# A state-space block with its norm moved to token rows, its scan cut into quarters, its skip term folded into the tables, and its outputs evicted through gelu

## The reference

```python
for i in range(2):
    x = x + 0.5 * swiglu(rmsnorm(x, ffn1_norm[i]), ffn1_w_in[i], ffn1_w_out[i])
    h = rmsnorm(x, mix_norm[i])
    x = x + (s5_mixer(h, ...) if i == 0 else hgrn2_mixer(h, ...))
    x = x + cross_attend(rmsnorm(x, xattn_norm[i]), mem_k[i], mem_v[i], ...)
    x = x + 0.5 * swiglu(rmsnorm(x, ffn2_norm[i]), ffn2_w_in[i], ffn2_w_out[i])
# s5_mixer: 64 groups of 16 channels, each driving a 64-dim complex diagonal state
h_t = lam_bar * h_{t-1} + b_bar @ u_t
y_t = gelu(real(c @ h_t) + d * u_t)
out = (y @ w_glu)[:, :1024] * sigmoid((y @ w_glu)[:, 1024:])
```

## Time and profile before

| | us |
|---|---|
| median of 3 runs | 2545.58 |
| the profiled execution, its own time | 2546.63 |
| its span | 2544.9 |
| PE busy | 2462.6 (97% of the span) |
| DVE busy | 1258.5 |
| ACT busy | 853.5 |
| POOL busy | 612.7 |

### The profile page before, as it was taken

One profiled execution on the slowest core, in us unless ns is written; L12 is line 12 of the kernel. 1 busy time (PEld: TensorE's weight loads), 2 busy tenths in 40 slices (PEclk: granted clock), 3 DMA queues, 4 the chain that ended last, 5 costly groups with the idle time before them and its releaser, 6 DMA issues.

```text
span 2544.9 us, 49720 instructions
## 1 busy us (share of the span) xinstructions
PE 2462.6 (97%) x21037; PEld 2370.9 (93%) x21037; DVE 1258.5 (49%) x1764; ACT 853.5 (34%) x1228; POOL 612.7 (24%) x604
## 2 busy tenths in 40 slices
PE   6999999799999999999999999999998999999999
PEld 6999999688976999999999999999998959999998
DVE  4553543854555543344543244466776565442443
ACT  3332221443222322222333133266664233221222
POOL 5579948241201100001211010331122203000003
PEclk8999999899999999999999999999999999999999
DMA  8255444363354333233443333333332543332332
GB/s 163 84 165 128 123 123 147 104 201 107 110 196 133 91 91 105 79 90 100 143 117 114 99 92 107 92 86 101 94 103 63 200 158 89 93 101 86 90 99 76
DMA packets 479670, 289.16 MB, mean 114 GB/s; under 512 B 22352, under 2 KB 467024, under 8 KB 478480
## 3 DMA queue, kind: packets, MB, share of 16 engines
q1 hardware_dynamic: 473760, 280.66, 37.6%
q0 software_dynamic: 848, 1.89, 0.7%
q10 hardware_dynamic: 4896, 4.20, 0.5%
HBM read 258.86 MB, written 27.85 MB: 113 GB/s over the span
## 4 chain that ended last, share of the span: by engine, by line
PE 91%; DVE 4%; ACT 2%; DMA 1%; issue 1%; POOL 1%; SPq 0%; DVEq 0%; ACTq 0%; POOLq 0%
PE lin L2670 76%; PE mis L2237 3%; DMA raw<-in_ffn_w_in_dram 1%; PE mis L2358 1%; DVE w_lo L1668 1%; DVE rstd L1681 1%; PE mis L2343 1%; PE mis L2293 1%; PE lin L2358 1%; PE mis L2523 1%; PE mis L2515 0%; PE lin L2601 0%; POOL w_lo L975 0%; DVE a_lo L1674 0%; DVE kc L1726 0%
## 5 line engine op out<-in xcount | busy, mean ns | idle before, releaser
L2670 PE MATMUL lin<-a_hi,w_hi 128*128 128x260 f32 x3584 | 1023.9, 286 | 18.9 <-DVE w_lo L1668 15.0
L2670 PE MATMUL lin<-a_lo,w_hi 128*128 128x260 f32 x3584 | 1015.8, 283 | 0.0
L2670 PE MATMUL lin<-a_hi,w_lo 128*128 128x260 f32 x3584 | 1015.2, 283 | 0.0
L2670 PEld LDWEIGHTS lin<-a_hi,w_hi 128*128 128x128 f32 x3584 | 677.1, 189 | 25.6 <-issue 12.8
L1668 DVE TENSOR_TENSOR w_lo<-raw,w_hi 128x1024 fp32r<-128x1024 f32 (+1 forms) x328 | 499.1, 1522 | 403.8 <-ACT w_hi L1239 403.4
L2670 PEld LDWEIGHTS lin<-a_hi,w_lo 128*128 128x128 f32 x3584 | 678.2, 189 | 0.0
L2670 PEld LDWEIGHTS lin<-a_lo,w_hi 128*128 128x128 f32 x3584 | 677.9, 189 | 0.2
L2670 PE MATMUL lin<-h_hi,w_hi 128*128 128x260 f32 x2016 | 570.1, 283 | 4.6 <-DVE h_lo L1898 1.7
L2670 PE MATMUL lin<-h_hi,w_lo 128*128 128x260 f32 x2016 | 569.3, 282 | 0.0
L2670 PE MATMUL lin<-h_lo,w_hi 128*128 128x260 f32 x2016 | 568.5, 282 | 0.0
L1239 ACT ACTIVATE w_hi<-raw 128x1024 fp32r<-128x1024 f32 (+1 forms) x328 | 364.5, 1111 | 320.1 <-PE lin L2670 300.0
(11 more groups left out here) (453 smaller groups left out, 2586.9 us busy)
## 6 DMA issues: line engine op xcount, KB each, us to landing
raw<-in_ffn_w_in_dram SPq DMA_DIRECT2D x176, 512.0 KB, 3.8
raw<-in_ffn_w_out_dram SPq DMA_DIRECT2D x64, 704.0 KB, 4.6
kc<-in_cache_mem_k_dram SPq DMA_DIRECT2D x32, 512.0 KB, 5.3
vc<-in_cache_mem_v_dram SPq DMA_DIRECT2D x16, 1024.0 KB, 8.6
raw<-in_hg_w_in_dram SPq DMA_DIRECT2D x32, 512.0 KB, 4.1
raw<-in_xattn_w_kv_dram SPq DMA_DIRECT2D x16, 512.0 KB, 4.3
raw<-in_s_w_glu_dram SPq DMA_DIRECT2D x16, 512.0 KB, 4.0
raw<-in_xattn_w_q_dram SPq DMA_DIRECT2D x16, 512.0 KB, 4.0
```

The lines of the kernel that those rows point to most:

```text
L2670: ins = pe.matmul(lin[:, j, half, 0:HT], w[:, j, k, :], x[:, k, cols], start=k == 0 and u == 0, stop=k == kt - 1 and u == 2)
```

## The change

- **Norm.** ACT packs tiles 0 to 6 from `xT` times gain, without the reciprocal, while `ffn1_out1` still runs (a new `sZ` of six tiles, and `sZ6`); DVE packs tile 7. ACT squares tile 7 and DVE adds it to POOL's sum. PE sums over channels into one column per step, so that the sums stand by token rows (80 x 8), after the sixth X group. Root and reciprocal are taken on 80 x 8, and the reciprocal is multiplied in when an X group is emptied (DVE six groups of eight, ACT two, in four pieces each).
- **Order.** X, U of the first half; X of the second; then FU of the first half, h0, U and FU of the second. Waits for all groups at the start of U and FU become waits for the groups that are read.
- **Scan** in four quarters with a signal for each; hfin comes later; Y(4,1) goes to ACT.
- **Skip term.** POOL makes `dD`, d on a 16-wide diagonal, and PE adds it to each K group with four more products of 16 columns per group. y needs no u any more: ACT empties y groups through gelu into `u32`.
- **kv.** The eight products with `w_lo` come last in a step, and only they wait for it (both layers). POOL's `kv_low` waits for the reciprocal.
- **Transfers.** Three tables instead of two are fetched ahead; the rotation tables, kv loads and memory tiles are fetched in another order. Root and gelu tables are loaded ahead by ACT on a spare element.

The list of groups:

```diff
+    sZ = at("sZ", [P, 6, CS, UC], F32, o_al)
+    sZ6 = at("sZ6", [P, CS, UC], F32, o_small + 2048 + 3 * TILE)
+    X_OWNER = ("dve", "act", "dve", "dve", "act", "dve", "dve", "dve")
     for hf in range(2):
-        made += [("X", (4 * hf + f, e), "act") for f in range(4) for e in range(2)]
...
+        made += [("X", (4 * hf + f, e), X_OWNER[2 * f + e]) for f in range(4) for e in range(2)]
         if hf == 0:
+            made += [("U", q, "dve" if q % 2 else "act") for q in range(8)]
+    made += [("FU", q, "dve" if q % 2 else "act") for q in range(8)] + [("h0", 0, "dve")]
+    made += [("U", 8 + q, "act") for q in range(8)] + [("FU", 8 + q, "act") for q in range(8)]
+    made += [("Y", (u, g), "act") for u in range(4) for g in range(2)]
+    made += [("y", (f, e), "act") for f in range(4) for e in range(2)]
```

SP:

```diff
-                sp.wait_ge(s5_z, 1)
-                rotation_in(0, "S")
-                kv_memory(0)
-                sp.wait_ge(s5_fill, S5G.at("X", (7, 1)) + 1)
+                sp.wait_ge(s5_fill, 1)
                 rotation_in(1, "C")
                 rotation_in(1, "S")
-                for c in (2, 3):
-                    kv_load(0, c)
+                sp.wait_ge(sums_done, s5_norm + 1)
+                rotation_in(0, "S")
+                kv_load(0, 2)
+                sp.wait_ge(s5_fill, S5G.at("X", (5, 1)) + 1)
+                rotation_in(0, "C")
+                kv_load(0, 3)
+                kv_memory(0)
```

ACT:

```diff
+                for f in range(7):
+                    act.wait_ge(used[f % 2], p0 + f // 2 + 1)
...
+                    act.activation(z[:, :, 0:NC], xT[:, f, 0:SEQ].rearrange("p (n s) -> p s n", s=CS), ACT.Copy, scale=gain)
...
+                act.activation(t2[:], xT[:, KD - 1, :], ACT.Square).then_inc(s5_packed, 1)
+                kv_split(0, 1)
                 act.wait_ge(sums_done, s5_norm + 1)
...
+                        act.activation(u32[:, f, 0:SEQ].rearrange("p (n s) -> p n s", s=CS)[:, :, 4 * e:4 * e + 4],
+                                       bank[:, 0:4 * YC].rearrange("p (t n) -> p n t", t=4)[:, 0:NC, :],
+                                       ACT.Gelu_apprx_tanh).then_inc(s5_void["act"], 1)
+                        if e:
+                            hidden({5: range(3), 6: range(3, 5), 7: range(5, KD)}.get(f, ()))
```

DVE:

```diff
+                        dve.tensor_tensor(dst, src, scale.unsqueeze(2).unsqueeze(3).to_broadcast([UC, 4, 8, SC]), ALU.mult)\
```

PE:

```diff
-                pe.wait_ge(kv_lo, v + 1)
+                pe.wait_ge(kv_hi, v + 1)
...
+                for u, (w, x) in enumerate(((kv_his[l], m_hi[l]), (kv_his[l], m_lo[l]), (kv_los[l], m_hi[l]))):
+                    if u == 2:
+                        pe.wait_ge(kv_lo, v + 1)
+                    for k in range(KD):
...
+                            ins = pe.matmul(bank[0:2 * SC, u * P:u * P + SC], ident[:, 2 * SC * u:2 * SC * (u + 1)],
+                                            dD[:, a, :], start=False, stop=True)
...
-                sums(s5_norm)
-                pe.wait_ge(root_done, s5_norm + 1)
...
+                    for k in range(CS):
+                        pe.matmul(mis[0:NC, 2, k:k + 1], acc[:, 0:SEQ].rearrange("p (n s) -> p s n", s=CS)[:, CS - 1 - k],
+                                  ones[:, 0:1], start=True, stop=True)
+                    pe.matmul(mis[NC:UC, 2, 0:CS], accS[:].rearrange("p a b -> p (a b)"), ones[:, 0:CS],
+                              start=True, stop=True).then_inc(sums_done, 1)
...
-                            pe.wait_ge(s5_scanned, 1 + u // 4)
+                            pe.wait_ge(s5_scanned, 1 + u // 2)
```

More of the change, by code:

```diff
@@ L763, in s5_loads @@
                 sp.wait_ge(s5_rot_out, 16 * 4)
-                rotation_in(0, "C")
-                for q in range(2):
+                for q in range(3):
                     s5_tables_in(q)
@@ L991, in body @@
                             continue
-                        if last and j == 1 and r == NORMS - 1:
+                        if last and j == 1 and r in (s5_norm, NORMS - 1):
                             continue
@@ L995, in body @@
                         ins = pool.tensor_tensor(acc[:], acc[:], sqt[:], ALU.add)
-                        if last and j == (0 if one or r == NORMS - 1 else 1):
+                        if last and j == (0 if one or r in (s5_norm, NORMS - 1) else 1):
                             ins.then_inc(squares_done, 1)
@@ L1457, in s5 @@
                         kv_tokens(0, KV - 1)
-                        gelu(5)
-                        hidden(range(3))
                         continue
@@ L1463, in s5 @@
                         continue
-                    if what == "X" and a[0] >= 4 and a[1] == 0:
-                        for f in (4, 5) if a[0] == 4 else range(a[0] + 1, min(a[0] + 2, KD)):
-                            packed(f)
                     act.wait_ge(s5_fill, q + 1)
@@ L1469, in s5 @@
                     if what == "X":
[L1470 to L1472 removed]
+                        if a[0] >= 4:
                             act.wait_ge(s5_fill, G.first("U") + 8)
[L1474 to L1477 removed]
+                        dst, src, scale = x_rows(a, bank)
+                        for u in range(4):
+                            ins = act.activation(dst[:, u], src[:, u], ACT.Copy, scale=scale[:, u:u + 1])
+                        ins.then_inc(s5_void["act"], 1)
+                        continue
+                    if what == "U":
                         dst, src = sU[:, 4 * a:4 * a + 4, :], bank[:, 0:4 * UC].rearrange("p (g n) -> p g n", g=4)
@@ new lines, in turn @@
+                    dve.tensor_tensor(x[:, 0], a[:, 0], b[:, 1], ALU.subtract if back else ALU.add)
+                    link(dve.tensor_tensor(x[:, 1], a[:, 1], b[:, 0], ALU.add if back else ALU.subtract))
+                for f in range(2):
+                    turn(f, False)
+                    q_ = slice(f * nj // 2, (f + 1) * nj // 2)
+                    j_ = slice(half * nj + f * nj // 2, half * nj + (f + 1) * nj // 2)
+                    for e in range(2):
+                        x = sFH[:, e, j_, :].rearrange("p j n -> p (j n)")
+                        link(dve.tensor_tensor_scan(x, rotR[:, q_].rearrange("p j n -> p (j n)"), x, 0.0, ALU.mult, ALU.add))
+                    if half == 0 and f == 1:
+                        dve.tensor_copy(rotR[:, :, 2:NC + 1], decay[:, nj:].unsqueeze(2).to_broadcast([P, nj, NC - 1]))
+                    turn(f, True)
+                    link(dve.tensor_copy(hfin[:, :, j_], sFH[:, :, j_, NC]))
+                    link(dve.tensor_copy(sFH[:, :, j_, NC:YC], hs0[:, :, :, j_].rearrange("p e b j -> p e j b")))
+                    dve.nop().then_inc(s5_scanned, 1)
```

219 lines of the change are left out of this document (102 added, 117 removed).

## The result

The change takes 2526.59 us (median of 4 runs, 2524.20 to 2528.02) against 2545.86 (4 runs, 2544.36 to 2548.33) for the kernel before on the same chip: ratio 0.9922, 95% interval 0.9907 to 0.9936. That is 19.3 us less. A second series of the same kernel gave a ratio of 0.9942 (0.9928 to 0.9957), so the gain is known as some 15 to 20 us and not to the microsecond.

The account below looks back on a forecast made before the run. PE was taken as the bound, busy 2462.6 of 2544.9 us. Front -14.3, K products +2.4 and back +1.6 sum to -10.3 us: 2535.3 us for a median, own range 2531 to 2540, whole range 2527 to 2543.

Parts of the forecast that it names:

- the list of steps: Front, feed-forward's end to first kv product: X, sums, U, FU timed in turn; at full clock kv starts 18.3 us earlier.
- Front, -14.3: From the feed-forward's last product to the first kv product: 18.3 us saved at full clock, less 4 for a clock fall.
- a fall that lasts for about 8 us costs 4: Front: PE, fed in drops from 449.5 to about 461, drops to the lower clock for about 8 us, losing 4.
- K products, +2.4: K groups: 64 added matmuls in the trace, at FU's pace of 0.037 us each, count in full on PE: +2.4 us.
- Back, +1.6: From the first kv product to the start of `glu`: net loss of 1.6 us, from -2 to +8.
- kv(2): -1.9: Third kv step, back: with the `w_lo` products last, 16 matmuls cover 1.9 of the 2.03 us wait.
- y(0) to y(3), +1.0: Back, ahead of Y(4): ACT empties y through gelu at 0.5 us each; PE's wait of 0.64 becomes 1.6.
- SP's tables, +1.4: Back: SP is held by a kv load, so Y(3)'s tables may come late like Y(2)'s: +1.4 us (-0.4 to +6).
- The end, +1.1: Behind the last Y: ACT alone needs 4.5 us until `glu` may start, against 3.4 when shared with DVE.
- the quarters themselves bring nothing: Scan in quarters, back: no gain, since the scan is off the path and three kv steps (11 us) hide Y(0)'s quarter.
- Of the rivals, the first: No fall of the clock and the queues hold: -19.1 us in all, 2526.5 us; chance 0.2.
- The second, low clock throughout: Clock stays low through the front, which gains only 4.0 us: total 0, 2545.6 us; chance 0.1.

## Why the prediction was wrong

The main mechanism was right: the chain behind the feed-forward goes, X starts at once, and the end moves by what the front loses. The steps that failed are the back, where the sum has a loss and the kernel gained, and in the front the cost of the fall of the clock and the list of steps. All three terms of the sum were mis-sized on the slow side.

- **Front, -14.3; measured -18.0, and about -17 in the mean of nine profiles** (against 46.90; the other profile with the front of before has 48.27, at 27.3 us of low clock). The sum stood for a front of 32.6 from start to start: 28.6 for the steps at full clock and 4.0 for the fall. Measured were 28.0 and a stall of 0.86 that nothing foretold. Of the 28.0 some 1.5 are the fall, which was 3.4 us long and not 8, and 26.5 the steps (estimates, with 0.43 us for each us of half clock). So "a fall that lasts for about 8 us costs 4" was too dear by 2.5, of which 2.0 is the length. That is luck: in the mean of nine profiles it was 7.6 us, and would then cost 3.3. The list was too long by 2.1. Its first steps weren't: the sums took 2.2 us, not 1.3, and the scale came 5.6 after the feed-forward's end, not 5.2. But the second U took 3.4 us, not 4.3, and the second FU 4.6, not 4.9. I took 0.5 for ACT to empty a U group; it lasts 0.44 and starts every 0.32. The rest of the 2.1 lies between the scale and the first FU product, where the clock falls and the estimate is rough.
- **K products, +2.4; measured +1.8.** FU's pace, 0.037, was too dear for 16 columns: 0.029.
- **Back, +1.6; measured -4.1,** which is the largest miss. kv(2): -1.9 was right for the wait, but 0.62 for the keys showed behind it: -1.4. y(0) to y(3), +1.0: nothing. I took 0.5 for a gelu of half a tile; it starts every 0.26. SP's tables, +1.4: 0.4 less in this profile, and 0.7 to 1.0 of wait in five of the other ten traces whose transfers are the change's. A wait of 0.32 for evicted values, which the sum left out, is gone too. The end, +1.1: -0.4 up to the first `glu` product and -1.5 behind it. I added up ACT's work as one row and left out that DVE, once it no longer empties y, runs `h_lo` ahead. The 0.61 us between the first weight tiles of `glu` stood in the trace of before, just behind the window that I had read.

Points of the forecast's own list: X within 0.3 us, right; scale 5 us after, 5.6; first kv product near 481.4, at 478.90; the low stretch, 3.4 us in place of 8; K groups +0.23, not 0.3; `w_lo`'s wait gone, right; Y(4) 1 us later, wrong. Two readings in it are off by a little: by their own shares (0.73 and 0.59) the clock before fell at 449.5 and 480.2, not at 449.7 and 480.4, so what is called 3 us of idleness at full clock was 2.8. The list has the two FU blocks at 4.65 and 4.9 us, where its row gives 4.7 for each; that moves the sum by 0.2. The remark that "the quarters themselves bring nothing" was wrong: the sum did not rest on it, but without the quarters some 60% of the gain would be lost. Of the rivals, the first had the time right, with -18.0 + 1.8 - 4.1 behind it in place of its -18.3 + 1.2 - 2.0, so it came out for a part of its reasons: the clock did fall, for 3.4 us. The second, low clock throughout, was refuted: between 457 and 461 PE ran only transposes, and the clock rose from 0.50 to 0.98 at 460. The Trainium skill (TensorE: Matmul & The Clock Gate, Part 4: PE-mode transpose) has full clock not engage there; this trace disagrees again. Of the others, SP's queue cost at most 1.0 us, the K products pipelined, and the scale was not late.

## What to carry to other kernels

Charge a fall of the clock a little under half its length where PE sets the pace (0.43 and 0.44 here), and less where another engine does (0.2). Its length is a matter of chance, so give it a spread and not a value. Before a price is taken from two executions of the same code, compare them stage by stage for a stall that only one of them has. For a row of operations on ACT count the distance of their starts and not what one of them lasts. When work moves off an engine, ask what that engine does next, and read the trace past the last wait: a consumer that runs slowly shows as busy, not as waiting. A stage that is shortened brings its successors forward against whatever did not shorten; look for the part (here the cut of the scan) that has to move too.

## What the runs showed of the hardware

- The low stretches in the front of one and the same code were 3.4, 6.8 and 10.2 us long; nothing in between was seen, nor in the front's variants.
- A product with one column is not cheap: 16 with 64 stationary columns, read 8 elements apart, start 0.126 us apart (2417), while those with 80 columns in FU start 0.035 apart (2.21 us for 64, from 466.17 to 468.38). Which of the two, the one column or the distance of 8, makes them slow isn't shown.
- A DVE operation on two SBUF tiles stood still while POOL had one of its own (3.39 us for 1.22), and so did a copy from SBUF to SBUF (2.20 for 0.17); POOL's split took 3.32 instead of 2.48 behind a DVE operation. DVE's emptying of X, with a PSUM input, wasn't touched (0.69).
- ACT's operations overlap: emptying 128 x 320 lasts 0.44 us and starts every 0.32, gelu of 128 x 256 out of PSUM lasts 0.38 to 0.49 and starts every 0.26.
